# PEER gates of the first 128 tokens through indirect DMAs into device memory, and no high-low pairs

## The reference

```python
q = (h @ wq).reshape(B, S, PEER_HEADS, 2, half).astype(f32)
s1 = jnp.einsum('bshd,hnd->bshn', q[..., 0, :], keys[:, 0].astype(f32))
s2 = jnp.einsum('bshd,hnd->bshn', q[..., 1, :], keys[:, 1].astype(f32))
v1, i1 = lax.top_k(s1, PEER_TOPK)
v2, i2 = lax.top_k(s2, PEER_TOPK)
cand = (v1[..., :, None] + v2[..., None, :]).reshape(B, S, PEER_HEADS, PEER_TOPK * PEER_TOPK)
sc, j = lax.top_k(cand, PEER_TOPK)
...
experts = e1 * PEER_NKEYS + e2
gates = jax.nn.softmax(sc, axis=-1)
...
act = jax.nn.gelu(jnp.einsum('td,ted->te', ht, u[et]), approximate=False)
return jnp.einsum('te,ted->td', gt * act, v[et])
```

## Time and profile before

| what | value |
|---|---|
| timed runs | 2362.66 to 2363.53 us, median 2362.92 us |
| profiled execution, first to last instruction | 2361.0 us |
| TensorE, weight loads, VectorE, ScalarE, GpSimd | 99%, 90%, 74%, 58%, 20% of it |
| moved | 421.77 MB, 179 GB/s on average |

### The profile page before, as it was taken

How to read it: one execution, slowest core, us unless ns; L and a number is a source line. 1 busy time by engine, 2 the same in 40 slices (tenths; PEclk the granted TensorE clock), 3 DMA queues, 4 the chain that set the end, 5 groups by cost and what they waited for, 6 DMA issues and landing times.

```text
span 2361.0 us, 40110 instructions
## 1 busy us (share of the span) xinstructions
PE 2335.1 (99%) x15655; PEld 2115.9 (90%) x15655; DVE 1755.3 (74%) x3335; ACT 1367.7 (58%) x2622; POOL 463.4 (20%) x411
## 2 busy tenths in 40 slices
PE   8999999999999999999999999999999999999999
PEld 8899999999888888888999999998888888899998
DVE  7967999788777777667599988885555555747864
ACT  6664445777655555566544467775554454666643
POOL 4720000788300000011000038870000000003000
PEclk9999999999999999999999999999999999999999
DMA  7234565444588888732266654446666675334452
GB/s 279 88 131 127 181 187 178 148 131 134 186 269 263 270 262 269 281 144 109 94 187 184 181 172 132 134 134 205 194 192 194 195 234 200 140 113 174 179 193 75
DMA packets 93283, 421.77 MB, mean 179 GB/s; under 512 B 10324, under 2 KB 12956, under 8 KB 85160
## 3 DMA queue, kind: packets, MB, share of 16 engines
q1 hardware_dynamic: 92784, 418.84, 54.6%
q10 hardware_dynamic: 312, 0.37, 0.0%
HBM read 415.98 MB, written 3.18 MB: 178 GB/s over the span
## 4 chain that ended last, share of the span: by engine, by line
PE 91%; DVE 6%; ACT 2%; DMA 1%; issue 1%; ACTq 0%; DVEq 0%
PE PS L170 90%; DVE r_sl L191 2%; DVE mem L191 1%; DVE mem L199 1%; ACT mem L181 1%; ACT r_sh L181 1%; DMA mem<-in_v 1%; PE PS L173 0%; DVE mem L205 0%; DVE mem L211 0%; DMA cst<-in_cst 0%; DVE r_gl L199 0%; DVE hT L199 0%; ACT L188 0%; DVE mem L195 0%
## 5 line engine op out<-in xcount | busy, mean ns | idle before, releaser
L191 DVE TENSOR_TENSOR r_sl<-mem,r_sh 128x1024 fp32r<-128x1024 f32 (+2 forms) x750 | 896.4, 1196 | 452.8 <-ACT r_sh L181 450.8
L181 ACT ACTIVATE r_sh<-mem 128x1024 fp32r<-128x1024 f32 (+2 forms) x750 | 767.5, 1024 | 493.9 <-PE PS L170 408.0
L170 PE MATMUL PS<-r_h,r_sh 128*128 128x256 f32 (+2 forms) x4800 | 752.6, 304 | 6.3 <-ACT r_h L181 2.8
L170 PEld LDWEIGHTS PS<-r_h,r_sh 128*128 128x128 f32 (+1 forms) x4800 | 647.5, 191 | 42.5 <-issue 8.9
L196 POOL TENSOR_SCALAR xT<-cst,mem 128x128 f32<-128x128 f32 x256 | 328.3, 1294 | 543.4 <-ACT mem L181 492.9
L170 PE MATMUL PS<-r_h,r_sl 128*128 128x256 f32 (+1 forms) x2832 | 400.7, 283 | 1.2 <-DVE r_sl L191 1.1
L170 PEld LDWEIGHTS PS<-r_h,r_sl 128*128 128x128 f32 (+1 forms) x2832 | 371.7, 191 | 10.9 <-DVE r_sl L191 2.2
L181 ACT ACTIVATE mem<-PS 128x256 f32<-128x256 f32 (+19 forms) x468 | 158.9, 351 | 324.1 <-PE PS L170 322.5
L170 PE MATMUL PS<-r_sh,r_ch 128*128 128x512 f32 x1024 | 276.1, 390 | 2.2 <-ACT r_sh L181 2.2
L170 PE MATMUL PS<-r_sh,r_cl 128*128 128x512 f32 x1024 | 274.8, 389 | 0.0
L170 PE MATMUL PS<-r_sl,r_ch 128*128 128x512 f32 x1024 | 274.7, 389 | 0.0
(11 more groups left out here) (170 smaller groups left out, 2504.4 us busy)
## 6 DMA issues: line engine op xcount, KB each, us to landing
mem<-in_u SPq DMA_DIRECT2D x256, 512.0 KB, 3.6
mem<-in_v SPq DMA_DIRECT2D x256, 512.0 KB, 4.4
mem<-in_w SPq DMA_DIRECT2D x16, 2048.0 KB, 8.2
mem<-in_ada SPq DMA_DIRECT2D x48, 512.0 KB, 4.9
mem<-in_in SPq DMA_DIRECT2D x9, 2048.0 KB, 8.8
mem<-in_wq SPq DMA_DIRECT2D x8, 2048.0 KB, 7.7
mem<-in_od_in SPq DMA_DIRECT2D x6, 2048.0 KB, 9.7
mem<-in_ev_in SPq DMA_DIRECT2D x5, 2048.0 KB, 14.4
```

Of the source, the lines that this page charges most:

```text
L170: return self.did(self.e and self.e.matmul(out, lhsT, rhs, start=start, stop=stop, skip_group_check=skip))
L181: return self.did(self.e and self.e.activation(out, in_, func, **kw))
L191: return self.did(self.e and self.e.tensor_tensor(out, a, b, op))
```

## The change

The dense gates of tokens 0 to 127 no longer come from one-hot products. A buffer `gd` of 16384 x 128 floats in device memory (8 MB a layer) is filled with zeros by 16 stores of 512 KB, issued by SP behind every second tile of u from tile 4 on, from a part of `xTf` that GpSimd sets to zero. VectorE makes the indices `IX` (expert x 128 + token) and the normalised gates `GX` as soon as the first half's choices are made; for this, ScalarE takes the exponential of that half in block 28. GpSimd then issues 128 indirect DMAs, one for each of a token's choices, which add one element to `gd` for each of 128 tokens; it waits for the landing of all before at each 16th. 48 come before its first hot matrix and three after each of the first hot matrices. SP loads `gd` back in 32 blocks of 128 x 512 floats (256 KB), block 0 behind tile V[1], blocks 1 to 3 behind V[3], the others each fourth v tile, and VectorE multiplies each into `av` (`gated_first`), block 0 in the last block of u, the others in every fourth block of v.

The one-hot groups are left for tokens 128 to 255: 32 of them, spread over blocks 78 to 124, from the last token down. GpSimd makes one hot matrix of a group, ScalarE one or two, VectorE the rest. One set of transposes (before block 76) is left. `PAIRED` is empty: all blocks of u are made of 24 products of 256 columns. Some semaphores of the last layer are merged.

```diff
+    def scatter_add(self, out, index, in_):
+        at = bass.IndirectOffsetOnAxis(ap=index, axis=0)
+        return Done(self, self.e and self.e.indirect_dma_start(out, at, in_, None, compute_op=ADD), 16)
...
+        io[f"gd{layer}"] = nc.dram_tensor(f"gd{layer}", (16384 * 128, 1), F32, kind="Internal").ap()
...
-    eT = [cbuf[:, 256 * i:256 * i + 256] for i in range(5)]
+    eT = [cbuf[:, 128 * i:128 * i + 128] for i in range(5)]
+    GX, IX = cbuf[:, 640:768], cbuf[:, 768:896].bitcast(U32)
+    gtile = [cbuf[:, 1024:1536]] + [hhi_raw_r[:, 512 * i:512 * i + 512] for i in range(3)]
...
-    AFTER = [C_FROM + g * (C_TO - C_FROM) // 64 for g in range(64)]
+    NG = 32
+    AFTER = [C_FROM + g * (C_TO - C_FROM) // NG for g in range(NG)]
+    FIRST_TOKEN = [124 - 4 * g for g in range(NG)]
+    ZEROED = 16
-    PAIRED = range(C_FROM + 2, 126)
+    PAIRED = range(0)
...
             for i, (src, freed, _) in enumerate(tiles):
...
                 sp.wait_ge(*freed)
                 sp.dma_start(raw[i % 4], src).then_inc(f"raw{i % 4}", layer, i)
+                if 4 <= i < 4 + 2 * ZEROED and i % 2 == 0:
+                    sp.wait_ge("zero", "gd", layer)
+                    sp.dma_start(pieces_of_gd[(i - 4) // 2], xTf[:, 0:1024]).then_inc("gz", layer, (i - 4) // 2)
+                elif i == v_at[1]:
+                    sp.wait_ge("scat", layer, 127)
+                    gate_blocks(0)
+                elif i == v_at[3]:
+                    sp.wait_ge("wdone", U[127])
+                    for n in range(1, 4):
+                        gate_blocks(n)
+                elif i in v_at and i >= v_at[7] and (v_at.index(i) + 9) % 4 == 0 and (v_at.index(i) + 9) // 4 < 32:
+                    n = (v_at.index(i) + 9) // 4
+                    sp.wait_ge("gated", layer, "first", n - 3)
+                    gate_blocks(n)
...
         def peer_po(po):
             norm_po(po, k, gain)
             po.wait_ge("x_out", layer)
-            for g in range(64):
-                s = 4 * (g % 2)
-                po.wait_ge("eT", layer, g // 32)
+            po.memset(xTf[:, 0:1024], 0.0).then_inc("zero", "gd", layer)
+            def scattered():
+                po.wait_ge("gz", layer, ZEROED - 1)
+                po.wait_ge("gates", layer, 0)
+                for n in range(128):
+                    if n and n % 16 == 0:
+                        po.wait_ge("scat", layer, n - 1)
+                    po.scatter_add(io[f"gd{layer}"], IX[:, n:n + 1], GX[:, n:n + 1]).then_inc("scat", layer, n)
+                    yield
+            scatter = scattered()
+            for _ in range(48):
+                next(scatter)
+            for g in range(NG):
+                n = FIRST_TOKEN[g]
+                po.wait_ge("eT", layer)
                 if g >= 2:
                     po.wait_ge("prod", layer, g - 2)
-                for i in range(2):
-                    n = 4 * g + i
-                    d = po.tensor_scalar(oneA[:, s + i, :], iota, eT[0][:, n:n + 1], EQ, eT[2][:, n:n + 1], MUL)
-                d.then_inc("hotP", layer, g)
+                po.tensor_scalar(oneA[:, 4 * (g % 2), :], iota, eT[0][:, n:n + 1], EQ, eT[2][:, n:n + 1], MUL).then_inc("hotP", layer, g)
+                for _ in range(3):
+                    next(scatter, None)
...
-                if j == C_FROM - 8:
-                    ac.wait_ge("gmax", layer)
-                    ac.activation(GT, GT, ACT.Exp).then_inc("gexp", layer)
+                if j in (28, C_FROM - 8):
+                    t = int(j > 28)
+                    ac.wait_ge("gmax", layer, t)
+                    w = GT[:, 128 * t:128 * t + 128]
+                    ac.activation(w, w, ACT.Exp).then_inc("gexp", layer, t)
...
         def hots_ac(ac, g):
-            for i in (2, 3) if g % 4 == 1 else (2,):
-                n, a = 4 * g + i, oneA[:, s + i, :]
+            for i in (1,) if g % 2 else (1, 2):
+                n, a = FIRST_TOKEN[g] + i, oneA[:, s + i, :]
...
         def coef_high(ac, j):
+            if j % 4 == 0:
+                ac.wait_ge("gated", layer, "first", j // 4)
...
+                if t == 0:
+                    ve.wait_ge(*d)
+                    ve.wait_ge("col", 0)
+                    ve.wait_ge(*ve.tensor_scalar(half(E1, 0), half(EF, 0), 128.0, MUL, C("tok"), ADD).then_inc("dveC"))
+                    ve.wait_ge(*ve.tensor_copy(IX, half(E1, 0)).then_inc("dveC"))
+                    normalised(0, GX).then_inc("gates", layer, 0)
+                    yield 15
...
+            def gated_first(i):
+                ve.wait_ge("gelu", layer, 4 * i + 3)
+                ve.wait_ge(*gate_block_in(i))
+                w = av[:, 4 * i:4 * i + 4, 0:128]
+                ve.tensor_tensor(w, w, gtile[gslot(i)].rearrange("p (j t) -> p j t", j=4), MUL).then_inc("gated", layer, "first", i)
...
+                if j == 127:
+                    gated_first(0)
...
+                if j % 4 == 1 and j < 124:
+                    gated_first(j // 4 + 1)
```

More of the change, by code:

```diff
@@ L100, in constants @@
     put("cneg", np.where(ok > 0, 0.0, NEG))
+    put("tok", p)
     return c
@@ L286, in declare @@
     io["xs"] = nc.dram_tensor("xs", (128, 2048), F32, kind="Internal").ap()
+    for layer in range(2):
+        io[f"gd{layer}"] = nc.dram_tensor(f"gd{layer}", (16384 * 128, 1), F32, kind="Internal").ap()
     return io
@@ L1417, in peer_ac @@
                 elif j >= J_LATE:
-                    ac.wait_ge("eT", layer, 1)
+                    ac.wait_ge("eT", layer)
                 if j in PAIRED:
@@ L1469, in coef_high @@
             if j == 0:
-                ac.wait_ge("hotP", layer, 63)
-                ac.wait_ge("hot", layer, 63)
-                ac.wait_ge("gated", layer, 63)
+                ac.wait_ge("hotP", layer, NG - 1)
+                ac.wait_ge("hot", layer, NG - 1)
+                ac.wait_ge("gated", layer, NG - 1)
+            if j % 4 == 0:
+                ac.wait_ge("gated", layer, "first", j // 4)
             if AHEAD[j]:
@@ L1494, in choices, with normalised @@
         def choices(ve):
-            g, s = GT.rearrange("p (h k) -> p h k", h=16), SC.rearrange("p (h k) -> p h k", h=16)
+            half = lambda a, t: a[:, 128 * t:128 * t + 128]
+            def normalised(t, out):
+                g = half(GT, t).rearrange("p (h k) -> p h k", h=8)
+                ve.wait_ge("gexp", layer, t)
+                ve.wait_ge(*ve.tensor_reduce(st[:, 0:8], g, ADD).then_inc("dveC"))
+                ve.wait_ge(*ve.reciprocal(st[:, 8:16], st[:, 0:8]).then_inc("dveC"))
+                return ve.tensor_tensor(out.rearrange("p (h k) -> p h k", h=8), g,
+                                        st[:, 8:16].rearrange("p (h o) -> p h o", o=1).broadcast_to([128, 8, 16]), MUL)
             for t in range(2):
@@ L1528, in choices @@
                 d = ve.tensor_copy(p16f, p16).then_inc("dveC")
-                if t:
-                    ve.tensor_tensor(g, s, s[:, :, 0:1].broadcast_to([128, 16, 16]), SUB).then_inc("gmax", layer)
+                g, s = (half(a, t).rearrange("p (h k) -> p h k", h=8) for a in (GT, SC))
+                ve.tensor_tensor(g, s, s[:, :, 0:1].broadcast_to([128, 8, 16]), SUB).then_inc("gmax", layer, t)
                 hv = hot.rearrange("p (k c) -> p k c", k=16)
@@ L1575, in hots @@
                     ve.wait_ge("prod", layer, g - 2)
[L1576 to L1579, removed]
+                ve.wait_ge("eT", layer)
+                first = FIRST_TOKEN[g]
+                for i in (2, 3) if g % 2 else (3,):
+                    n = first + i
+                    ve.tensor_scalar(oneA[:, s + i, :], iota, eT[0][:, n:n + 1], EQ, eT[2][:, n:n + 1], MUL)
                 ve.tensor_tensor(oneB[:, s:s + 4, :], iota.rearrange("p (o e) -> p o e", o=1).broadcast_to([128, 4, 128]),
-                                 eT[1][:, 4 * g:4 * g + 4].rearrange("p (t o) -> p t o", o=1).broadcast_to([128, 4, 128]),
+                                 eT[1][:, first:first + 4].rearrange("p (t o) -> p t o", o=1).broadcast_to([128, 4, 128]),
                                  EQ).then_inc("hot", layer, g)
@@ L1587, in gate_tile @@
                     ve.wait_ge("gelu", layer, j)
-                    ve.tensor_tensor(av[:, j, 0:n], av[:, j, 0:n], gtmp[:, j % 2, 0:n], MUL).then_inc("gated", layer, "tile", j)
+                    ahead = av[:, j, 256 - n:256]
+                    ve.tensor_tensor(ahead, ahead, gtmp[:, j % 2, 0:n], MUL).then_inc("gated", layer, "tile", j)
+            def gated_first(i):
[3 more added lines that the diff above has]
+                ve.tensor_tensor(w, w, gtile[gslot(i)].rearrange("p (j t) -> p j t", j=4), MUL).then_inc("gated", layer, "first", i)
             for j in range(128):
@@ L1592, in peer_ve @@
                     ve.wait_ge("x_out", layer)
+                    ve.wait_ge("gz", layer, ZEROED - 1)
                     hots(0)
```

93 lines of the change are left out of this document (49 added, 44 removed).

## The result

The changed kernel takes 2444.38 us (median; 2442.82 to 2448.64), against 2363.23 us (2362.66 to 2364.31) for the kernel before beside it: ratio 1.0342, interval [1.0328, 1.0357]. It is 81 us slower; I had forecast 44 us faster, and the range ended at 2425 us. Rival A is what happened, with a higher price than I gave it.

The account below looks back on a forecast made before the run. TensorE, busy 99% of the span, was taken as the bound. Terms -49.2 - 0.7 + 1.8 + 3 + 0.6 + 0.3 = -44.2 us on the 2361.0 us span gave 2316.8 us, 2319 us as timed; range 2308 to 2425.

Parts of the forecast that it names:

- Rival A: Blocks 78 to 124: GpSimd becomes the bound, hot matrix behind three DMAs of 1.86 us; 2419 us, 2422 with loads; chance 0.33.
- What bounds the kernel, and what goes from TensorE: Blocks 78 to 127: bound by TensorE alone; 32 of 64 groups go, 197.5 to 172.9 us, 24.6 us a layer.
- The price s of an indirect DMA: GpSimd's time for one indirect DMA, taken as 1.2 us; TensorE waits from 1.19 us, whole gain gone at 1.50 us.
- The formula for the lateness: Group stretch: TensorE is late by 78 s + W - 104.7 us a layer, predicted 0.9 us a layer.
- W: GpSimd's waits on landings at each 16th DMA, four between the groups: 8 to 19 us, 12 taken.
- The first 48 hidden: Before the first hot matrix: 48 DMAs have 115 us, hidden up to 2.4 us each.
- rival B: DMA engines are the bound at 0.222 us an element (lower price 0.06): 159 us a layer, some 2635 us; chance 0.06.
- Zeroing, ScalarE's table change: During u: zeroing stores cost zero, at worst 2 us a layer; table change at block 28 costs 0.3 us in two layers.
- The start of the products with v: End of u: SP's gate block loads delay V[4] by 1 to 2 us; 0.3 us a layer taken.
- The end of the row of 128: SP's wait behind V[1]: with s = 1.2 the 128th DMA is issued near block 118, seven blocks ahead.
- Products with v in layer 0: 32 added loads of 256 KB beside the ada tiles: 3 us taken, 0 to 8 possible.
- The Trainium skill's rule weighed in the prediction: GpSimd's DMA issue, locked out by VectorE's two-port copies, goes from 620 to 3100 ns; at 3.1 us some 300 us slower.

Follow-up runs that it names:

- e1_hots_off: The changed kernel with GpSimd's hot matrices moved to VectorE, so the indirect DMAs follow each other on GpSimd; 2341.65 us, 0.9908 against the kernel before.
- e3_no_add: The changed kernel with indirect DMAs that write their element in place of adding it; 2440.17 us median, 1.0323 against the kernel before.
- e7_no_side: e1_hots_off with VectorE leaving out the maxima, indices and replacements of the second 128 tokens' keys; one run, 2344.41 us.
- e12_one_input: e7_no_side with VectorE's cuts of blocks 36 to 51 made a multiplication by zero with one SBUF input; one run, 2325.23 us.
- e4_none: The changed kernel with all 256 indirect DMAs left out, zeroing and gate loads kept; 2317.24 us, 0.9800 against the kernel before.
- e9_pace: e1_hots_off with VectorE making the choices 6% faster from block to block; 2325.88 us, 0.9845 against the kernel before.

## Why the prediction was wrong, point by point

- **What bounds the kernel, and what goes from TensorE**: right. 172.9 us predicted for blocks 78 to 127, 172.6 us busy in e1_hots_off. The transposes: 406.56 to 424.23 us is 17.67 us, where 18.00 stood before (406.27 to 424.27 us), 0.33 as predicted.
- **The price s of an indirect DMA: the step that failed.** I took 1.2 us, from GpSimd's mean for another instruction and SP's longest issue. Measured: 1.79 us as mean of 256, and 0.30 us behind each that I had not counted at all, so 2.09 us; in the group stretch 1.69 + 0.30. It has three parts: 0.95 us for 128 plain elements, 0.59 us for the adding form (e3_no_add), and up to 1.04 us of waiting where it begins in certain operations of VectorE (e7_no_side, e12_one_input), 0.15 and 0.64 us as means of two stretches. The first two have nothing to do with the durations of the rows that I leaned on the earlier trace rows. I had worked out that 1.50 us was the turning point, and the value that I took lay 0.3 us below it on no evidence for an adding DMA. The third part could have been read from the trace of the kernel before. There a hot matrix of GpSimd takes 0.79 us alone and 1.82 us when it begins in a cut, and it ends 0.67 us after the cut's end; most of the spread of the earlier trace rows is such waiting:

```profile
433.43 1.23 DVE L191 TENSOR_TENSOR r_sl<-mem,r_sh 128x1024 fp32r<-128x1024 f32 x1 [0.58 <-ACT r_sh L181]
433.50 1.82 POOL L196 TENSOR_SCALAR xT<-cst,mem 128x128 f32<-128x128 f32 x1
...
436.67 0.79 POOL L196 TENSOR_SCALAR xT<-cst,mem 128x128 f32<-128x128 f32 x1
```

- **The formula for the lateness**: right in its form. With the measured price and W it gives 78 x 1.99 + 10.1 - 104.7 = 60.6 us, measured 62.1; it held at a second price (e3_no_add). That the term of 1.29 us for a hot matrix fits is in part luck: hot matrices 0 to 26 took 1.78 us as mean, but the profile has each begin some 0.5 us before the end of the indirect DMA in front of it, so that 1.25 us of the period are left for it.
- **W, the waits on landings**: 12 us taken, 3.59 + 2.56 + 0.88 + 3.08 = 10.1 us measured. A fifth one, behind the first hot matrix, I had not counted; it took 0.73 us.
- **The first 48 hidden**: right. They end at 422.35 us, 1.5 us before the choices are there.
- **DMA engines (rival B)**: 36,864 packets took 4.0% of 16 x 2440.8 us, 0.042 us each, under the lower of my two bounds. The Trainium skill's sentence on transfers under 512 B (DMA: Bandwidth & Descriptors, section "Specifications") gives no time. I had drawn from it that the price would be nearer to the upper bound, and that is not borne out.
- **Zeroing, ScalarE's table change**: free, as said. TensorE waits 0.3 us in all from 198 to 424 us.
- **The start of the products with v**: 0.3 us a layer taken, for SP's loads; the first product waits 1.09 us in each layer of e4_none, and not for SP. VectorE's gate product of block 0 comes behind its last cut of u, and ScalarE's first cut of `av` waits for it. I had put VectorE's gate products at zero.

```profile
597.03 0.69 DVE L194 TENSOR_TENSOR mem<-mem 128x512 f32<-128x512 f32 x1
597.83 0.42 ACT L184 ACTIVATE r_ch<-mem 128x256 fp32r<-128x256 f32 x1 [1.98 <-DVE mem L194]
```

- **The end of the row of 128**: that it would be close to the end of u I had said (block 118, seven blocks ahead), but with s = 1.2; at 2.09 it ends behind u even when nothing else is on GpSimd.
- **Products with v in layer 0**: 3 us taken; from first product with v to the first of the next stage 357.7 us before, 359.4 after, 361.6 in e4_none.
- **The Trainium skill's rule weighed in the prediction** (SBUF — State Buffer, section "SBUF: two separate sides", the lock by a copy with two ports) pointed the right way. Its 3.1 us would be 250 us over the kernel before; the "some 300 us slower" of the prediction holds against the forecast. In the changed kernel the longest wait came from the cut with two inputs, 2.58 us in all. The one-input multiplication of e12_one_input held the DMA up to its end too; whether it runs in the mode with two ports no view here tells.
- **Range and chances**: A was given 0.33 and its price was GpSimd's longest instruction, 1.86 us. The range was cut at s = 1.88 although the bound that I had named from above was 3.6 us; the measured 1.99 us between the groups lies beyond it.

Not tried: a looser wait than on all DMAs before at each 16th. It stands there because two heads of a token can choose the same expert, so that two DMAs add to one element. What a looser wait would bring, and whether the sums would stay right, no run shows.

## What to carry to other kernels

An engine that is busy for 20% of the span (and for 83% of the stretch that matters) is not free for what an order written out by hand puts in front of its urgent work: here 80 DMAs stood ahead of 27 small matrices that TensorE waited for, and moving the matrices to another engine was worth 103 us. Where a change issues an instruction that no trace has shown, work out the price at which the gain is gone, and if it lies between the bounds, say that the sign is open; here it was 1.50 us between 0.33 and 3.6. And add up a row of such instructions to its end: even off the path of the groups it came 12 us late for the next stage.

## What the runs showed of the hardware that I had not expected

- An indirect DMA of 128 single elements holds GpSimd for 0.95 us as a plain write and for 1.54 us when it adds, the shortest of each; 0.30 us pass before the next. The adding form shows 144 packets for each, the plain one 32. When it begins during a VectorE operation with two inputs from SBUF, or during the one-input multiplication of e12_one_input, it ends about 1.42 us after that operation's end, which makes up to 2.58 us in the changed kernel (two of e9_pace took 2.96 and 3.03 us). An operation with one input from SBUF and one from PSUM, and a reduction, did not hold it up (1.55 us). With the cuts the two engines can fall into step and meet in each block.
- After the wait of TensorE of 3.46 us at 445 us, 16 products took 3.76 us where they take 2.16 us, at a granted clock of 0.50.
- Plain indirect writes went with late tiles of u (9.17 MB moved from 300 to 380 us against 14.76 MB), in one profiled execution; adding ones did not. The cause is open.
